# One two-layer decoder kernel: bare items one in five, the value copy first in Vector's round, the output projection's sums dealt out, and the last gates and norm by halves

## What is computed

```python
# layer 0: gated short convolution and latent attention, one output projection
hc, gc, gb, cq, ckv, kpe = _split_last(a @ w_in, (CONV_W, CONV_W, CONV_W, Q_RANK, KV_RANK, ROPE_DIM))
up = jnp.concatenate([conv_prev, gc * hc], axis=1)
conv = conv_w[0] * up[:, 0:t]
for k in range(1, CONV_K):
    conv = conv + conv_w[k] * up[:, k:k + t]
y_conv = gb * conv
...
y_att = jnp.einsum('bthr,rhv->bthv', o_lat, w_uv).reshape(b, t, N_HEADS * V_DIM)
y = jnp.concatenate([y_conv, y_att], axis=-1) @ w_out
# the end of every layer, and the last norm
gate = jax.nn.sigmoid(_rms(h, prm['norm_ple'][i]) @ prm['w_ple_gate'][i])
h = h + gate * (p[i] @ prm['w_ple'][i])
...
return _rms(h, prm['norm_f'])
```

## Time and profile before

| | |
|---|---|
| median of 3 runs | 1509.54 us (1509.47 to 1510.04) |
| the profiled execution, its own time | 1511.34 us |
| its span in the profile | 1509.5 us |
| PE busy | 1465.8 us, 97% |
| DVE busy | 1014.6 us, 67% |
| ACT busy | 272.9 us, 18% |
| POOL busy | 103.3 us, 7% |
| DMA, mean | 102 GB/s |

### The profile page before, as it was taken

How to read it: one execution, slowest core, us unless ns; L and a number is a source line. 1 busy time by engine, 2 the same in 40 slices (tenths; PEclk the granted TensorE clock), 3 DMA queues, 4 the chain that set the end, 5 groups by cost and what they waited for, 6 DMA issues and landing times.

```text
span 1509.5 us, 18900 instructions
## 1 busy us (share of the span) xinstructions
PE 1465.8 (97%) x7042; PEld 1176.1 (78%) x7042; DVE 1014.6 (67%) x2066; ACT 272.9 (18%) x575; POOL 103.3 (7%) x114
## 2 busy tenths in 40 slices
PE   8999999899999999999999999999999999999996
PEld 6756676588888888888877778788888888888885
DVE  3654444777866766766847777787766766767845
ACT  4132212122001001011233321121001011011232
POOL 0224332000000000000200002200000000000100
PEclk9999999899999999999999999999999999999998
DMA  6558865222222222222213121122222222222201
GB/s 270 161 157 253 235 208 179 90 82 84 84 84 84 84 84 84 84 84 99 83 51 123 56 84 56 60 84 84 84 84 84 84 84 84 80 76 90 78 29 59
DMA packets 40700, 154.25 MB, mean 102 GB/s; under 512 B 6753, under 2 KB 19458, under 8 KB 27810
## 3 DMA queue, kind: packets, MB, share of 16 engines
q1 hardware_dynamic: 35490, 136.27, 26.3%
q0 software_dynamic: 5120, 16.78, 3.7%
HBM read 150.01 MB, written 3.02 MB: 101 GB/s over the span
## 4 chain that ended last, share of the span: by engine, by line
PE 92%; DVE 5%; issue 1%; DMA 1%; ACT 0%; DVEq 0%; SPq 0%
PE psum L610 70%; PE psum L580 7%; PE psum L716 6%; PE psum L801 1%; PE psum L909 1%; PE psum L851 1%; PE psum L565 1%; DMA ring<-in_weights 1%; PE psum L941 1%; PE psum L674 0%; PE psum L866 0%; PE psum L765 0%; PE psum L918 0%; DVE arena L1332 0%; PE psum L992 0%
## 5 line engine op out<-in xcount | busy, mean ns | idle before, releaser
L610 PE MATMUL psum<-arena 128*128 128x272 f32 x2016 | 480.6, 394 | 0.0
L610 PEld LDWEIGHTS psum<-arena 128*128 128x128 f32 x2016 | 383.7, 191 | 79.5 <-DVEq L1328 0.6
L1332 DVE TENSOR_TENSOR arena<-psum,arena 128x272 f32<-128x272 f32 x564 | 248.8, 441 | 243.6 <-PE psum L610 220.2
L610 PE MATMUL psum<-B,ring 128*128 128x272 f32 x736 | 186.0, 395 | 4.3 <-issue 2.3
L610 PE MATMUL psum<-arena,ring 128*128 128x272 f32 x672 | 167.7, 392 | 0.0
L610 PEld LDWEIGHTS psum<-B,ring 128*128 128x128 f32 x736 | 139.4, 191 | 34.1 <-issue 3.6
L610 PE MATMUL psum<-A,ring 128*128 128x272 f32 x608 | 152.6, 393 | 1.6 <-DVE A L1838 1.5
L610 PEld LDWEIGHTS psum<-arena,ring 128*128 128x128 f32 x672 | 127.4, 190 | 26.0
L610 PEld LDWEIGHTS psum<-A,ring 128*128 128x128 f32 x608 | 115.4, 190 | 26.0 <-DVE A L1838 2.0
L1061 ACT ACTIVATE arena<-psum 128x272 f32<-128x272 f32 x84 | 33.3, 396 | 548.2 <-PE psum L610 548.2
L610 PE MATMUL psum<-B,arena 128*128 128x272 f32 x368 | 92.5, 392 | 0.0
(11 more groups left out here) (246 smaller groups left out, 1376.1 us busy)
## 6 DMA issues: line engine op xcount, KB each, us to landing
ring<-in_weights SPq DMA_DIRECT2D x98, 1024.0 KB, 4.8
arena<-in_keys SPq DMA_DIRECT2D x128, 144.0 KB, 3.2
h<-in_xT SPq DMA_DIRECT2D x8, 544.0 KB, 8.5
out_yT<-A SPq DMA_DIRECT2D x8, 272.0 KB, 2.3
arena<-in_attw SPq DMA_DIRECT2D x1, 1536.0 KB, 17.5
arena<-in_wuq SPq DMA_DIRECT2D x1, 1216.0 KB, 14.3
arena<-in_pemb SPq DMA_DIRECT2D x2, 544.0 KB, 5.9
ring<-in_weights SPq DMA_DIRECT2D x2, 512.0 KB, 6.2
```

Of the source, the lines that this page charges most:

```text
L610: end = pe.matmul(bank(g, n), lhs[:, c, :], x(c), start=c == 0, stop=c == 3)
L1332: ins = dve.tensor_tensor(out, bank(g, n), more, ALU.add)
```

## The change

Four things are changed. (1) The bare items are 5, 10, 15, 20, 25, 29, 30, 31 in place of 6, 13, 21, 27, 28, 29, 30, 31; the convolution's parts are moved by about one item, and in a DVE round the scaling of the last half tile comes ahead of the convolution's part. (2) In even rounds DVE's copy of the values comes first in the round and not last. (3) DVE makes the first 240 columns of the token sums of pair 2 in round 25, the weight sums in rounds 26 and 27, the token sums of pair 0 in round 29 and of pair 1 in round 31; PE runs the first chunk of P2 at n = 31. (4) In layer 1 the tiles g6 and g7 are computed as g6 first half, g7 first half, g6 second half, g7 second half, and all that hangs on them, down to the norm, its spreading and the stores, is done for the first half of the tokens and then for the second: 16 stores of 136 KB, and on ACT a table load for the first root, one back to the sigmoid's table and one again to the root's.

```diff
@@ -74,10 +73,10 @@
-BARE = (6, 13, 21, 27, 28, 29, 30, 31)
+BARE = (5, 10, 15, 20, 25, 29, 30, 31)
 HALF_AT = dict(zip([n for n in range(32) if n not in BARE], range(N_HALVES)))
-CONV_STEPS = {0: {7: 0, 8: 1, 9: 2, 10: 3}, 1: {14: 0, 15: 1, 16: 2, 17: 3}, 2: {21: 0, 22: 1, 23: 2, 24: 3},
-              3: {28: 0, 29: 1, 30: 2, 31: 3}}
+CONV_STEPS = {0: {6: 0, 7: 1, 8: 2, 9: 3}, 1: {13: 0, 14: 1, 15: 2, 17: 3}, 2: {20: 0, 21: 1, 22: 2, 23: 3},
+              3: {27: 0, 28: 1, 29: 2, 30: 3}}
...
@@ -481,10 +488,16 @@
+            def store(m, half):
+                sp.dma_start(a["yT"][m * P:(m + 1) * P, half], A[:, m, half]).then_inc(stored, 16)
+
+            for m in range(KD):
+                sp.wait_ge(dve_half, m + 1)
+                store(m, N1)
...
-                sp.dma_start(a["yT"][m * P:(m + 1) * P, :], A[:, m, :]).then_inc(stored, 16)
-            sp.wait_ge(stored, 80 + 16 * KD)
+                store(m, N2)
+            sp.wait_ge(stored, 80 + 32 * KD)
...
+            def last_gates():
+                t6, t7, v = T_PLE[1]["g6"], T_PLE[1]["g7"], U_PLE[1] + 4
+                def spread(i):
+                    pe.wait_ge(diag_ready, i + 1)
+                    pe.matmul(psum[:, B_SPREAD[i], 0:TH], ones[:], rstd[:, TH * i:TH * i + TH],
+                              start=True, stop=True).then_inc(spread_full, 1)
+
+                pe.wait_ge(w_loaded[v % SLOTS], 16 * (v // SLOTS + 1))
+                pe.wait_ge(dve_read, 6 * (G_GATE[1] + 1) + READ.index(P3) + 1)
+                free(t6)
+                half_tile(t6, 0, range(KD)).then_inc(half_full, 1)
+                free(t7)
+                half_tile(t7, 0, range(KD)).then_inc(half_full, 1)
+                half_tile(t6, 1, range(KD)).then_inc(psum_full, 1)
+                pe.wait_ge(dve_read, 6 * (G_GATE[1] + 2))
+                half_tile(t7, 1, range(1))
+                pe.wait_ge(half_summed, 1)
+                sums(0, ssum[:, :], True, True).then_inc(final_sums, 1)
+                half_tile(t7, 1, range(1, KD - 1))
+                spread(0)
+                half_tile(t7, 1, range(KD - 1, KD)).then_inc(psum_full, 1)
+                pe.wait_ge(half_summed, 2)
+                sums(1, ssum[:, :], True, False)
+                pe.wait_ge(half_squared, 4)
+                sums(1, sq[:, 1, :], False, True).then_inc(final_sums, 1)
+                spread(1)
...
@@ -921,8 +980,11 @@
-                if n == 32:
+                if n == 31:
                     pe.wait_ge(w_loaded[U_OUTAB % SLOTS], 16 * (U_OUTAB // SLOTS + 1))
+                    pe.wait_ge(half_free, N_HALVES)
+                    out_first(P2, range(1))
+                elif n == 32:
                     pe.wait_ge(conv_done, 1)
                     pe.wait_ge(pexp, 31)
...
-            pe.wait_ge(half_free, N_HALVES)
-            out_first(P2, range(2))
+            out_first(P2, range(1, 2))
             out_first(P6, range(2))
...
@@ -1017,18 +1078,6 @@
-            pe.wait_ge(dve_read, 6 * (G_GATE[1] + 2))
-            pe.wait_ge(sum_step, 55)
-            for x, last in ((ssum[:, :], False), (sq[:, 1, :], True)):
...
-            end.then_inc(final_sums, 1)
-            pe.wait_ge(diag_ready, 1)
-            ones_tile(T_NF, [rstd[:, :]])
...
@@ -1138,18 +1187,48 @@
+                if l:
+                    return last_gates(sigmoid, chunk)
...
+            def last_gates(sigmoid, chunk):
+                sigmoid(rbuf[:, 0, N1], 11)
+                chunk(5)
+                sigmoid(rbuf[:, 1, N1], 12)
+                act.wait_ge(h_done, H_GATE[1] + 7)
+                act.wait_ge(sum_step, 53)
+                squared(6, N1)
+                act.wait_ge(h_done, H_GATE[1] + 8)
+                act.wait_ge(sum_step, 54)
+                squared(7, N1)
+                scaled(6, N1)
+                scaled(7, N1)
+                sigmoid(rbuf[:, 0, N2], 13)
+                root(7, vn[:, 0:3])
+                act.wait_ge(h_done, H_GATE[1] + 9)
+                squared(6, N2)
+                scaled(6, N2)
+                act.activation(small[:, 93:94], ones[:, 0:1], ACT.Sigmoid)
+                act.wait_ge(spread_full, 1)
+                act.activation(rbuf[:, 0, N1], psum[:, B_SPREAD[0], 0:TH], ACT.Copy).then_inc(spread_copied, 1)
+                sigmoid(rbuf[:, 1, N2], 14)
+                act.activation(small[:, 94:95], ones[:, 0:1], ACT.Sqrt)
+                act.wait_ge(h_done, H_GATE[1] + 10)
+                squared(7, N2)
+                scaled(7, N2)
+                root(8, vn[:, 3:6])
...
@@ -1572,7 +1653,7 @@
                 if part == 0:
-                    dve.wait_ge(half_free, 6 * c + 6)
+                    dve.wait_ge(half_free, 6 * c + 4)
...
+                    dve.wait_ge(half_free, 6 * c + 6)
                     link(dve.tensor_tensor(acc, acc, gb, ALU.mult))
...
@@ -1661,22 +1743,23 @@
-                elif n == 28:
+                elif n == 25:
+                    dve.wait_ge(stored, 32)
+                    token_sums(B, XT_AB, 2, None, 0, TP - TH)
+                elif n in (26, 27):
+                    weight_sums(G_OUTAB, n - 26)
+                elif n == 29:
                     dve.wait_ge(st_full, N_BLOCKS)
                     dve.wait_ge(v_used, 13)
                     token_sums(B, XT_AB, 0, xt_ready)
-                elif n in (29, 30):
-                    weight_sums(G_OUTAB, n - 29)
-                elif n == 32:
+                elif n == 31:
                     token_sums(B, XT_AB, 1, xt_ready)
-                    dve.wait_ge(stored, 64)
-                    token_sums(B, XT_AB, 2, None, 0, TP - TH)
                 elif n == 33:
                     out_turned(1)
+                if n - 1 in HALF_AT:
+                    scaled_half(HALF_AT[n - 1])
                 if n in STEP_AT:
                     conv(*STEP_AT[n])
-                if n - 1 in HALF_AT:
-                    scaled_half(HALF_AT[n - 1])
...
@@ -1768,6 +1851,11 @@
             for n in range(NPR + 3):
+                if n >= 3 and n % 2 == 0:
+                    m = n - 3
+                    hd, i = item(m)
+                    dve.wait_ge(y_full, m // 2 + 1)
+                    dve.tensor_copy(B[:, 4 + hd // 2, i * P:(i + 1) * P], psum[:, 6, 0:P]).then_inc(y_free, 1)
...
@@ -1784,11 +1872,6 @@
-                if n >= 3 and n % 2 == 0:
-                    m = n - 3
-                    hd, i = item(m)
-                    dve.wait_ge(y_full, m // 2 + 1)
-                    dve.tensor_copy(B[:, 4 + hd // 2, i * P:(i + 1) * P], psum[:, 6, 0:P]).then_inc(y_free, 1)
...
@@ -1907,21 +1990,88 @@
+            def gate_scaled(m, i):
+                dve.tensor_tensor(rbuf[:, m - 6, half], slot(t)[:, i, 0:TH], rstd[:, half], ALU.mult).then_inc(gate_in, 1)
...
+            def gate_added(m, i):
+                link(dve.tensor_tensor(pp[1][:, m, half], pp[1][:, m, half], rbuf[:, m - 6, half], ALU.mult))
+                dve.tensor_tensor(h[:, m, half], h[:, m, half], pp[1][:, m, half], ALU.add).then_inc(h_done, 1)
...
+            def half_sum(m, half):
+                dve.wait_ge(half_squared, {(6, 0): 1, (7, 0): 2, (6, 1): 3}[m, int(half is N2)])
+                link(dve.tensor_tensor(ssum[:, half], ssum[:, half], sq[:, m % 2, half], ALU.add))
...
+            def variance(i):
+                dve.wait_ge(final_sums, i + 1)
+                link(dve.tensor_scalar(vn[:, 3 * i:3 * i + 2], psum[:, 2, 0:8:4] if i == 0 else psum[:, 0:4:2, 0],
+                                       1.0 / D, EPS, ALU.mult, ALU.add))
...
+            def diagonal(i):
+                n, b = TH - 2 * P, TH * i
+                dve.wait_ge(root_done, 8 + i)
+                dve.reciprocal(vn[:, 3 * i:3 * i + 3], vn[:, 3 * i:3 * i + 3]).then_inc(rstd_done, 1)
...
+                dve.tensor_tensor(rstd[:, b:b + 2 * P].rearrange("p (i n) -> p i n", i=2),
...
+            def out_first(*ms):
+                for m in ms:
+                    if m == 0:
+                        dve.wait_ge(spread_copied, 1)
+                    if m < 6:
+                        dve.wait_ge(x_ready, 48 + m + 1)
+                    else:
+                        dve.wait_ge(half_scaled, m - 5)
+                    dve.tensor_tensor(A[:, m, N1], A[:, m, N1], rbuf[:, 0, N1], ALU.mult).then_inc(dve_half, 1)
+            gate_scaled(6, 0)
+            sum_sq(6, 4)
+            gate_added(6, 0)
+            gate_scaled(7, 0)
+            sum_sq(6, 5)
+            gate_added(7, 0)
+            dve.wait_ge(gate_in, 13 + 12)
+            link(dve.memset(rstd[:, 2 * P:TH], 0.0))
             link(dve.memset(vn, 1.0))
-            link(dve.memset(rstd[:, TP:T], 0.0))
-            dve.wait_ge(final_sums, 1)
...
+            half_sum(6, N1)
+            half_sum(7, N1)
+            dve.nop().then_inc(half_summed, 1)
+            gate_scaled(6, 1)
+            variance(0)
+            gate_added(6, 1)
+            diagonal(0)
+            half_sum(6, N2)
+            dve.nop().then_inc(half_summed, 1)
```

(11 more changed lines are left out.)

80 lines of the change are left out of this document (52 added, 28 removed).

## The result

| | before | after |
|---|---|---|
| median of the runs beside the first profile | 1509.79 us (4 runs) | 1501.28 us (4 runs, 1498.57 to 1502.76) |
| the same in a later, longer comparison | 1509.54 us (26 runs, 1504.43 to 1511.96) | 1502.17 us (6 runs, 1498.82 to 1502.89) |
| the profiled execution, its own time | 1511.34 us | 1501.79 us |
| its span | 1509.5 us | 1500.0 us |

The ratio of after to before is 0.9947, 95% interval 0.9932 to 0.9962, and 0.9948 (0.9933 to 0.9963) in the longer comparison. So the kernel became 7.4 to 8.5 us faster. The forecast was 13.05, and its range ended at 1501.5 us: the first median lies 0.2 us inside it, the later one 0.7 us outside.

The account below looks back on a forecast made before the run. PE, busy 97% of the span, was taken as the bound, with gains only where it waits, is clocked low, or has finished. 9.8 + 3.25 = 13.05 us took the median from 1509.54 to 1496.5 us, range 1493.8 to 1501.5.

Parts of the forecast that it names:

- The two places: Attention loop's last items, 250 to 294 us, gain 9.8 us; behind PE's last large products, gain 3.25 us.
- the stages between unchanged in length: Between the attention loop and the start of g6: a sign expected in the new profile, no change in time.
- Item 20's wait: Attention loop, bare item 20: paged scores wait for the copy out of bank 4; 1.9 us, bounds 0 and 3.7.
- DVE's rounds 29 to 32: End of the attention loop, item 29's scores to the last paged sum: 4.7, 3.0, 3.4 and 2.4, sum 13.5 us.
- The next group: First output group behind the attention loop: starts at 290.4 in place of 300.20 us, a gain of 9.8 us.
- The value copy: Late attention loop: copying values first in DVE's round removes PE's waits of 4.91 and 2.65 us, costing 0.2 us per round.
- The end: From g6's start to the span's end: 28.7 us in place of 31.9, gain 3.25 us, bounds 1.3 and 4.
- the end gives nothing: Rival for the kernel's end: stores, table changes and more small steps eat the 3.25 us; 1499.7 us, chance 0.10.
- A table change costs twice its load: Rival for ACT at the end: standing still again behind each load, up to 2.6 us later; 1499.1 us, chance 0.02.
- The clock falls once more: Rival for the loop's last items: new waits bring a half-speed stretch costing up to 3.3 us; 1499.8 us, chance 0.22.
- the single price: ACT at the end: each table change costs only its load, 1.28 us, about 1.3 us, with no drain added.
- the median, which equals the span to 0.1 us: Whole kernel: the profiled span's gain of 13.05 us carried over to the median of runs, 1509.54 to 1496.5 us.

Follow-up runs that it names:

- copy last: Changed kernel with the copy of the values put back at the end of DVE's round; 1502.02 us, ratio to before 0.9945.
- both back: Changed kernel with the value copy last in its round and sums, weight sums and first products at their old items, new bare items kept; 1504.33 us.
- the end alone: Kernel before with only the change to the end (last gates, norm and stores by halves), loop as before; 1506.59 us, ratio 0.9987.
- long filling: Changed kernel with 9, 9 and 17 throwaway products ahead of PE's three waits of 880 to 952 us, outlasting them; 1505.21 us.
- The shifts: Changed kernel with 18 or 45 throwaway products in the first feed-forward stage, making everything behind 4.02 or 10.05 us later; 1502.73 and 1513.74 us.
- the short filling: Changed kernel with 5, 5 and 7 throwaway products ahead of PE's three waits of 880 to 952 us; 1497.90 us, ratio 0.9923.
- the last run: Changed kernel with items 21 and 27 bare for 20 and 29, second token sums at round 32, three later waits filled with 5, 5, 7 products; 1491.31 us.

## Why the prediction was right and where it was wrong

The two places that it named gave nearly what it said: the loop 9.30 us for 9.8, the end 2.94 for 3.25. What failed is the step "the stages between unchanged in length": the sum put them at nothing, and they took 3.51 us more, 3.19 in two more stretches at 1.2 GHz, 0.65 in a longer wait for DVE at 952 us, less 0.33 elsewhere. From span to span, 9.30 + 2.94 - 3.51 + 0.77 = 9.50 us; the 0.77 is the earlier start of that one execution, luck that the forecast did not count on.

- *Item 20's wait.* Forecast 1.9 us, measured 1.82, at the place named, and the loop without it is 1.78 us shorter. The four other new bare items show no wait, as forecast. What the step left out is that such a wait can be followed by low clock. Neither profile of after has that, but two others with the same loop do.
- *DVE's rounds 29 to 32.* Forecast 13.5 us, from item 29's scores to the last paged sum. Measured from 262.15 to 275.37 + 0.35 = 275.72: 13.57 us, with one gap of 0.50 that the forecast did not have, so that its steps were too long by about as much: the sum is right in part by luck. Item 29 starts at 261.24 instead of 262.0, and that is the earlier start of 0.77; from the early projections to item 29 the way grew by 1.88 us (1.9 forecast).
- *The next group.* Forecast 290.4, measured 290.13. That looks like 10.07 us for 9.8, but without the earlier start of 0.77 it is 9.30, half a microsecond less than forecast; 0.4 of it lies behind the last paged sum (275.72 to 290.13 is 14.41 us, 14.0 forecast). PE waits 0.47 + 2.11 + 0.97 + 0.74 = 4.29 us there (4.2 forecast, none over 2), and the clock stayed at 1.00 as forecast.
- *The value copy.* "It takes away both waits" is true of the kernel before, where that one edit removes both, but it is not what the gain hangs on. In the changed kernel copy last again costs nothing, and both back costs 4.07 us. The copy's place and the dealing of the sums are two cures for one wait, and only the sum over DVE's rounds, which I also made, was right to carry the gain.
- *The end.* Forecast 28.7 us from g6 to the end of the span, measured 28.98; a gain of 2.94 instead of 3.25, and 2.95 in the runs of the end alone. The last square starts at 1489.34, 18.32 us behind g6's start (18.47 forecast: 1496.05 - 1477.58). The multiplications took 2.87 us, not 2.65, and the span ends 3.25 us behind the last of them, not 2.94. The rival that the end gives nothing is out.
- *A table change costs twice its load.* It doesn't here. The activations start 0.02 us or less behind loads of 1.28 us, at 1486.70 and 1489.23 as in the earlier trace rows, and the end is 0.3 us from where the single price put it, not 2.6. The Trainium skill, page "ScalarE: Activation LUTs", section "What ACT_TABLE_LOAD costs", adds a drain of about 1380 ns to each change; the load's own time agrees with these rows, the drain does not.
- *The clock falls once more.* This rival, at 1499.8 us, had the right mechanism and the wrong place. I looked for the fall in the loop's last items, where the new waits are. It came 600 us later, behind waits in stages that the change does not touch, one of 1.14 us in both kernels and the one of 2.07 in place of 1.52. Against the rival I had held 828 to 834 us, where PE waits and the clock stays at 1.00. That one execution was a sample, not a property of the program: at the same place the clock fell in two other profiles (copy last, long filling), and before, too, has runs at 1504.0 to 1505.9 us, where most lie near 1509.7.
- *From the profile to the median.* The profiled execution of before took 1511.34 us, which is 1.8 us above the median of its kernel. An execution's own time is 1.8 us above its span in after too (1501.79 and 1500.0), so "the median, which equals the span to 0.1 us" was a chance agreement: the profiled execution was a slower one. I carried the 13.05 us over to the median whole. The gain of one profiled execution over the other is 9.55 us; from median to median it is 7.4 to 8.5. So the forecast lost 3.5 us by the profiles, and another 1 to 2 us because the profile of before was of a slower execution. That this one had more low stretches than the common one fits its mean clock (0.989, and 0.990 or 0.991 in most runs) but is not shown.

What stays open is the rule by which a wait is or isn't followed by low clock. The shifts show that a move in time changes which waits are followed, the short filling that the wait matters, and the last run that a wait isn't needed.

## What to carry to other kernels

A gain read off one profiled execution holds for the waits, but the granted clock in it is one draw: count the low stretches, price each (1.5 to 1.7 us here), and ask for every wait of over a microsecond, near the change or far from it, what happens when the change moves it in time. A wait on the busiest engine can be worth more than its length: without item 20's 1.8 us the median was 3.8 lower, though the other 2 us may have come with the shift. Compare the start of the first stage in both profiles before reading a gain off absolute times: 0.77 us of the 10.07 here lay ahead of the change. When two edits are said to remove a wait, take each back alone and both together before giving either the credit.

## What the runs showed of the hardware that I had not expected

- With nothing but a shift of 4.02 us (18 products in the middle of a stage that never waits), two stretches at the lower clock went in the profile and the median rose by 0.6 us only; with 10.05 us it rose by 11.6.
- Work added can make the kernel faster: 17 throwaway products in three waits took the median from 1502.17 to 1497.90 us.
- A product of 128 columns in fp32 takes 0.22 us of PE and shows as two instructions (90 of them for 45 products, 10.05 us), not half of that.
- The same two instructions, a multiplication of DVE's and a token sum of GpSimd's, take 0.99 and 0.77 us when GpSimd's begins 0.08 us ahead, and 0.44 and about 1.06 us when DVE's begins at that moment or 0.01 us ahead. In the first order PE's wait at 952 us is 2.05 to 2.08 us, in the second 1.52 (13 unfilled profiles). Shifts of 4 and 10 us left it at 2.08 and 2.06.
